# The gate products of a token mixer taken out of the mixer and run between the steps of gated linear attention

## Chip, cores, metric

One core of one Trainium2 chip. The metric is the device time of one execution in microseconds, the median of several executions.

## What is computed

One layer of a bidirectional encoder on 512 prompt tokens and 2048 sample tokens (2560 together, width 1024, all in f32). The part that matters here:

```python
(aq, ak, av, gq, gk, gv, gr, glf, glb, ga, gg) = split_cols(h @ p['w_in'][l])
attn = windowed_gqa(...)
la_f = jax.nn.log_sigmoid((glf @ p['gla_wa2_fwd'][l] + p['gla_ba_fwd'][l])) / GLA_GATE_NORMALIZER
la_b = ...                                    # the same for the other direction
o_f = gla_chunked(gq, gk, gv, la_f, False)
o_b = gla_chunked(gq[:, ::-1], gk[:, ::-1], gv[:, ::-1], la_b[:, ::-1], True)[:, ::-1]
o_g = rms_norm(o_f + o_b, p['gla_norm'][l]).reshape(B, S, GLA_VAL_WIDTH) * jax.nn.silu(gr)
merged = (jax.nn.sigmoid(ga) * (attn @ p['w_branch_attn'][l])
          + jax.nn.sigmoid(gg) * (o_g @ p['w_branch_gla'][l]))
return merged @ p['w_out'][l]
```

`ga` and `gg` are 1024 wide each: two products of `h` with 1024 columns of `w_in`. They need `h` alone, neither the attention nor its result. After this come a norm, the residual sum, a router and 16 experts.

## The kernel before

The kernel is written engine by engine: each phase is a block in which every engine (PE the matrix engine, ACT, DVE, POOL, and SP, which issues most loads) has its own list of instructions, run strictly in the order of the code; semaphores are the only ties between engines. Phases: the front (norm and modulation, `hT` stored), projections and windowed attention (`pa_`), gated linear attention (`gla_`), the mixer (`mix_`), routing, experts (`moe_`), the final norm.

An f32 product of full precision is written as three products of `fp32r` parts (`product3`, lines 103 to 105): high by high, high by low, low by high. So each weight and each input gets a high part (`w_hi`, `a_hi`: a cast on ACT) and a low part (`w_lo`, `a_lo`: raw minus high, on DVE).

`phase_gla` runs first backward over the tiles of 128 tokens (18 steps: a scan on DVE, exponentials on ACT, a turn of the keys and a product on PE, the state on DVE, kept in `Sb`), then forward over 20 tiles (slots). A slot of the forward pass on DVE: the scan of the next tile's decays (L1170), 24 small subtractions that make the arguments of the exponentials (`args`, L1139 to L1143), the state's arguments (L1179, L1180), the norm of the last output (L1201), five predicated copies that pick the levels out of PSUM (`level`, L1195), the product with q (`times_q`, L1186), the state (L1240) and the final product (L1208). ACT makes the exponentials (`exps`, L1257 to L1260), POOL the product with k (`times_k`, L1301), the mean squares' power (`rms`) and the store of `og`. PE makes the levels (L1362, L1371), the turn of the keys (L1379), the state's product (L1389) and the output (L1396 to L1402). Two PSUM tiles `p_g` take the levels in turn.

`phase_mix` runs over five blocks of 512 tokens in 20 chunks of weights each. Even chunks below 16 hold two pieces of 128 columns of `w_in` (for `ga` and `gg`, 48 products 512 wide), odd ones the two branch matrices (24 products 512 wide); chunks 16 to 19 hold 256 columns of `w_out` each (96 products 256 wide). ACT takes the sigmoid of the gates out of PSUM (L1610), DVE multiplies by the branches (L1695), sums (L1697), and the merged tile is split into `m_hi` (ACT, L1617) and `m_lo` (DVE, L1699). The norm, residual sum, squares, turn and router product of block b-1 (`post_a`, `post_b`, `post_c`) are spread over the chunks of block b. Weights have two buffers, `w_raw[m % 2]`: chunk m+1 is split while chunk m runs.

Of the kernel before, what the change touches and what calls it, by code (L numbers as in the profile page):

```python
# [14 lines left out]
P = 128  # L15
# [868 lines left out]
def phase_gla(nc, K, I, S):  # L884

# [4 lines left out]
    NG = NLEV - DIRECT  # L897
    with Mem(nc, "gla") as M:
# [6 lines left out]


# [14 lines left out]


        p_g = [M.ps(f"p_g{i}", [P, 2, 2, 2, P]) for i in range(2)]
# [3 lines left out]
        p_k, p_s = p_ks[:, 0:2], p_ks[:, 2:4]  # L927
        PAIRS = (NG + 1) // 2
        DVE_LEVELS = 6
        s_c, s_m, s_z = M.sem("consts_loaded"), M.sem("mask_step"), M.sem("zeroed")  # L930

# [13 lines left out]
        f_st = [M.sem(f"f_stored{i}") for i in range(2)]  # L945

        def toks(t):
            return bass.ds(t * P, P)
# [9 lines left out]

        with nc.Block() as block:
            @block.sync  # L960
            def _(sp):
                with nc.allow_non_contiguous_dma(reason="a small vector onto partitions"):
                    sp.dma_start(gnorm[:], I["gla_norm"].rearrange("b p -> p b")).then_inc(s_c, 16)
                sp.wait_ge(s_c, 16)

            @block.gpsimd
            def _(pool):
                pool.iota(ip[:], pattern=[[0, P]], base=0, channel_multiplier=1)
                pool.iota(it[:], pattern=[[1, P]], base=0, channel_multiplier=0).then_inc(s_m, 1)
                pool.memset(L[:], 0.0)  # L970

# [16 lines left out]
        with nc.Block() as block:  # L988
            def tiles(eng, tile):

                tile(0, 19, 0)
                tile(1, 18, 1)
                with eng.Fori(1, 7) as i:
                    tile(i * 2, 19 - i * 2, 0)
                    tile(i * 2 + 1, 18 - i * 2, 1)
                for n, t in ((14, 5), (15, 3), (16, 2), (17, 1)):
                    tile(n, t, n % 2)

            p_u = (p_o[:, 0], p_o[:, 1])

            @block.gpsimd
            def _(pool):
                pool.memset(Sf[:], 0.0)

            def is_left(n):

                return not isinstance(n, int) or n < 18

            @block.sync
            def _(sp):  # L1010
                def load_lk(n, t, u):
                    wait(sp, b_B, n - 1)
                    held(sp, K)
                    sp.dma_start(L[:, u, 2:4, 1:P + 1], S["la"][2:4, :, toks(t)].rearrange("c p n -> p c n")).then_inc(b_in[u], 16)
                    wait(sp, b_k, n - 1)
                    held(sp, K)
                    sp.dma_start(k[:, u], S["gk"][:, :, toks(t)].rearrange("c p n -> p c n")).then_inc(b_kin[u], 16)

                def tile(n, t, u):
                    if isinstance(n, int) and n == 0:  # L1020
                        load_lk(0, t, 0)
                    if is_left(n + 1):
                        load_lk(n + 1, 3 if isinstance(n, int) and n == 14 else t - 1, 1 - u)
                    wait(sp, b_p, n - 1)
                    held(sp, K)
                    sp.dma_start(v[:, u], S["gv"][toks(t), :]).then_inc(b_v[u], 16)
                tiles(sp, tile)

            @block.vector
            def _(dve):  # L1030
                def sums(n, u):
                    dve.wait_ge(b_in[u], (n - u) * 8 + 16)
                    wait(dve, b_e, n - 1)
                    dve.tensor_tensor_scan(B[:, u, 2:4].rearrange("p c n -> p (c n)"),
                                           keep[:, 2:4].rearrange("p c n -> p (c n)"),
                                           L[:, u, 2:4].rearrange("p c n -> p (c n)"), 0.0, ALU.mult, ALU.add).then_inc(b_B, 1)
# [76 lines left out]
        with nc.Block() as block:  # L1113
            def slots(eng, slot, last=None):
# [3 lines left out]
                if last:  # L1118
                    last()
# [1314 lines left out]
```

## Time and profile before

| | |
|---|---|
| median of 3 executions | 4129.35 us (4125.22 to 4130.35) |
| the profiled execution: time, span | 4131.49 us, 4129.9 us |
| PE busy | 3618.6 us (88%) |
| DVE busy | 2144.4 us (52%) |
| ACT busy | 1551.2 us (38%) |
| POOL busy | 478.6 us (12%) |
| mean granted clock of PE | 0.918 |
| bytes by DMA | 592.61 MB, mean 143 GB/s |

Busy times are sums over the whole span, and the stages differ: which engine a stage waits for has to be read stage by stage. The granted clock is a share of 2.4 GHz; 0.50 is the lower of its two levels, 1.2 GHz, and values between are means of both. Lengths of matmuls overlap; the pace of a run of them is read from start to start.

### The profile page before, as it was taken

The numbers are of one execution on the slowest core, as the hardware profiler recorded it, in microseconds if no ns is written. First come the engines' busy times: TensorE is split into PE (matmuls) and PEld (weight loads), VectorE is DVE, ScalarE is ACT, GpSimd is POOL, SyncE is SP. The second block draws the span as 40 slices with busy tenths as digits, with TensorE's granted clock in tenths as the row PEclk, the third lists the DMA queues.
The fourth block names the chain that finished last, engine by engine and source line by source line (L and its number), as shares of the span: only waits on it lengthen the run. The fifth ranks groups of instructions, "written<-read, shape, count | busy, mean of one in ns | idle before, by whom it ended". The sixth has DMA issues, their size and how long they took to land. (4 is left out here: it accounts for less than half of the span.)

```text
span 4129.9 us, 60082 instructions
## 1 busy us (share of the span) xinstructions
PE 3618.6 (88%) x22692; PEld 3049.2 (74%) x22692; DVE 2144.4 (52%) x3948; ACT 1551.2 (38%) x2274; POOL 478.6 (12%) x571
## 2 busy tenths in 40 slices
PE   7699999996566589999999963999999999999990
PEld 3377776764345478888888852999999999999990
DVE  1334444554899733444344425555555656555544
ACT  2334544553333233343334220444433443444442
POOL 0000100000344300000000010001000111010003
PEclk9799999997676789999999965999999999999995
DMA  8633343323222244454454432555555555555548
GB/s 286 226 118 104 104 130 97 104 88 97 80 78 65 79 114 143 130 156 138 133 153 143 148 130 72 164 167 171 168 161 164 157 173 169 164 180 160 165 135 328
DMA packets 537807, 592.61 MB, mean 143 GB/s; under 512 B 75640, under 2 KB 450456, under 8 KB 536736
## 3 DMA queue, kind: packets, MB, share of 16 engines
q1 hardware_dynamic: 506896, 474.84, 36.9%
q0 software_dynamic: 30016, 104.88, 8.3%
q10 hardware_dynamic: 720, 10.49, 0.6%
q8 instruction: 119, 1.95, 0.2%
q14 instruction: 56, 0.46, 0.0%
HBM read 484.23 MB, written 105.91 MB: 143 GB/s over the span
## 5 line engine op out<-in xcount | busy, mean ns | idle before, releaser
L103 PE MATMUL moe_pg<-moe_x_hi,moe_w_hi 128*128 128x320 f32 x2048 | 635.1, 310 | 1.4 <-DVE moe_x_lo L2195 1.4
L105 PE MATMUL moe_pg<-moe_x_hi,moe_w_lo 128*128 128x320 f32 x2048 | 633.4, 309 | 0.0
L104 PE MATMUL moe_pg<-moe_x_lo,moe_w_hi 128*128 128x320 f32 x2048 | 633.4, 309 | 0.0
L2157 DVE TENSOR_TENSOR moe_w_lo<-moe_w_raw,moe_w_hi 128x2048 fp32r<-128x2048 f32 x192 | 439.9, 2291 | 370.8 <-ACT moe_w_hi L2105 314.2
L1635 DVE TENSOR_TENSOR mix_w_lo<-mix_w_raw,mix_w_hi 128x2048 fp32r<-128x2048 f32 x100 | 186.4, 1864 | 493.4 <-ACT mix_w_hi L1560 493.4
L2105 ACT CAST moe_w_hi<-moe_w_raw 128x2048 fp32r<-128x2048 f32 x192 | 364.6, 1899 | 172.6 <-DMA moe_w_raw<-in_w_gate_e_dram 95.7
L103 PE MATMUL mix_pu<-mix_a_hi,mix_w_hi 128*128 128x512 f32 x960 | 380.4, 396 | 21.3 <-DVE mix_w_lo L1635 9.3
L103 PEld LDWEIGHTS moe_pg<-moe_x_hi,moe_w_hi 128*128 128x128 f32 x2048 | 385.1, 188 | 2.4 <-issue 1.5
L104 PEld LDWEIGHTS moe_pg<-moe_x_lo,moe_w_hi 128*128 128x128 f32 x2048 | 385.1, 188 | 0.6
L105 PEld LDWEIGHTS moe_pg<-moe_x_hi,moe_w_lo 128*128 128x128 f32 x2048 | 385.0, 188 | 0.0
L105 PE MATMUL mix_pu<-mix_a_hi,mix_w_lo 128*128 128x512 f32 x960 | 376.3, 392 | 0.0
L104 PE MATMUL mix_pu<-mix_a_lo,mix_w_hi 128*128 128x512 f32 x960 | 376.2, 392 | 0.0
L103 PE MATMUL pa_pu<-pa_h_hi,pa_w_hi 128*128 128x512 f32 (+1 forms) x560 | 227.9, 407 | 37.7 <-DVE pa_h_lo L644 37.7
L103 PEld LDWEIGHTS mix_pu<-mix_a_hi,mix_w_hi 128*128 128x128 f32 x960 | 182.0, 190 | 62.0 <-DVE mix_w_lo L1635 11.4
L104 PE MATMUL pa_pu<-pa_h_lo,pa_w_hi 128*128 128x512 f32 (+1 forms) x560 | 220.7, 394 | 0.0
L105 PE MATMUL pa_pu<-pa_h_hi,pa_w_lo 128*128 128x512 f32 (+1 forms) x560 | 220.6, 394 | 0.0
L105 PEld LDWEIGHTS mix_pu<-mix_a_hi,mix_w_lo 128*128 128x128 f32 x960 | 181.8, 189 | 38.6
L104 PEld LDWEIGHTS mix_pu<-mix_a_lo,mix_w_hi 128*128 128x128 f32 x960 | 182.1, 190 | 37.1
L103 PE MATMUL moe_pd<-moe_w_hi,moe_h_hi 128*128 128x512 f32 x512 | 203.2, 397 | 0.0
L105 PE MATMUL moe_pd<-moe_w_hi,moe_h_lo 128*128 128x512 f32 x512 | 199.7, 390 | 0.0
L104 PE MATMUL moe_pd<-moe_w_lo,moe_h_hi 128*128 128x512 f32 x512 | 199.5, 390 | 0.0
L103 PE MATMUL mix_pu<-mix_w_hi,mix_m_hi 128*128 128x256 f32 x640 | 182.2, 285 | 2.1 <-DVE mix_m_lo L1699 2.1
(309 smaller groups left out, 7104.1 us busy)
## 6 DMA issues: line engine op xcount, KB each, us to landing
moe_w_raw<-in_w_gate_e_dram SPq DMA_DIRECT2D x64, 1024.0 KB
moe_w_raw<-in_w_up_e_dram SPq DMA_DIRECT2D x64, 1024.0 KB
moe_w_raw<-in_w_down_e_dram SPq DMA_DIRECT2D x64, 1024.0 KB
mix_w_raw<-in_w_in_dram SPq DMA_DIRECT2D x80, 512.0 KB
pa_w_raw<-in_w_in_dram SPq DMA_DIRECT2D x35, 1024.0 KB
front_w<-in_w_ada_dram SPq DMA_DIRECT2D x24, 1024.0 KB, 11.8
mix_w_raw<-in_w_out_dram SPq DMA_DIRECT2D x20, 1024.0 KB
scratch_hT<-front_hT ACTq DMA_DIRECT2D x5, 2048.0 KB, 10.4
```

The costliest lines, as they stand in the source:

```text
L103: pe.matmul(out, w_hi, x_hi, start=start, stop=False)
L104: pe.matmul(out, w_hi, x_lo, start=False, stop=False)
L105: return pe.matmul(out, w_lo, x_hi, start=False, stop=stop)
L1635: dve.tensor_tensor(w_lo[:, m % 2, 0:n], w_raw[:, m % 2, 0:n], w_hi[:, m % 2, 0:n].bitcast(F32), ALU.subtract).then_inc(s_wlo, 1)
L2105: act.copy(w_hi[:, m % 2], w_raw[:, m % 2]).then_inc(s_whi, 1)
L2157: dve.tensor_tensor(w_lo[:, m % 2], w_raw[:, m % 2], w_hi[:, m % 2].bitcast(F32), ALU.subtract).then_inc(s_wlo, 1)
```

## The change

The 80 gate products (5 blocks, 8 column pieces, `ga` and `gg`) are taken out of the mixer. In `phase_gla` each is a `unit(n)` of 24 products, 512 wide, with `h` split once for a block and its 128 columns of weights split by ACT and DVE. Units 0 to 18 stand in the backward pass, one a step; unit 19 between the passes; three in each slot of the forward pass. ACT copies each unit out of PSUM (`read_unit`), POOL stores it to a scratch tensor `gate`. PSUM for this comes from the levels: `p_g` is now one tile. The subtractions, levels and norms of a slot on DVE are in another order, with the low parts of the weights between them, and the output of tile t-1 is made in slot t. The passes and the blocks of the mixer are written out, without register loops.

The mixer has 12 chunks a block: 8 with both branch matrices (24 products 512 wide) and 4 that hold half of the rows for 512 columns of `w_out` (48 products 512 wide). The gates are read back by SP into `sg`, 128x1024 at a time in two slots, and ACT takes the sigmoid in SBUF. `post_a` is at even branch chunks, `post_b` at odd ones.

```diff
+        def load_w(sp, n):
...
+            wait(sp, d_wlo, n - 1)
+            c0 = (C_GA, C_GG)[n % 2] + n % 16 // 2 * P
+            sp.dma_start(w_raw[:, n % 2], win[:, :, c0:c0 + P]).then_inc(d_w[n % 2], 16)
+        def load_h(sp, i):
+            wait(sp, d_hlo, 2 * i - 4)
...
+                def after_unit(n):
+                    if ends_block(n):
+                        split_h_lo(dve, (n + 1) // 16)
+                    split_w_lo(dve, n + 3)
...
+                for t in range(NT):
+                    n, w = FIRST_U + PER * t, 1 - t % 2
+                    more = t + 1 < NT
+                    if more:
+                        sums(t + 1)
+                        args(dve, w, 0)
+                        args(dve, w, 1)
+                    after_unit(n)
+                    level(t, 0)
+                    if more:
+                        args(dve, w, 2)
+                        args(dve, w, 3)
+                    if t:
+                        norm(t - 1)
+                    after_unit(n + 1)
+                    level(t, 1)
+                    level(t, 2)
+                    if more:
+                        args(dve, w, 4)
+                        args(dve, w, 5)
+                        state_args(t + 1)
+                    state(t)
+                    after_unit(n + 2)
+                    level(t, 3)
+                    level(t, 4)
+                    if t:
+                        final(t - 1)
+                    if more:
+                        times_q(t + 1)
...
+                def read_unit(n):
+                    act.wait_ge(d_u, n + 1)
+                    wait(act, d_st[n % SG], 16 * (n // SG))
+                    act.copy(sg[:, n % SG], pd[n % 2][:]).then_inc(d_ev, 1)
+                    if ends_block(n):
+                        split_h_hi(act, (n + 1) // 16)
+                    split_w_hi(act, n + 3)
...
+                    read_unit(n + 1)
+                    if t + 1 < NT:
+                        exps(t + 1)
+                    read_unit(n + 2)
...
+                for t in range(NT):
+                    n = FIRST_U + PER * t
+                    unit(n)
+                    if t:
+                        out(t - 1)
+                    pe.wait_ge(f_x, t + 1)
+                    pe.wait_ge(f_xq, t + 1)
+                    levels(t, 0)
+                    turn_keys(t)
+                    unit(n + 1)
+                    levels(t, 1)
+                    state_product(t)
+                    unit(n + 2)
+                    levels(t, 2)
+                    if t:
+                        turn_out(t - 1)
...
-    NM, NUB = 20, 40
+    NM, NUB = 12, 24
...
+                def load_gate(b, c):
+                    g = b * KD + c
...
+                    wait(sp, s_mlo, g - 1)
+                    sp.dma_start(sg[:, g % 2], S["gate"][2 * c:2 * c + 2, :, b * BLK:(b + 1) * BLK].rearrange("c p n -> p c n"))\
+                        .then_inc(s_g[g % 2], 16)
...
+                        load_w(b * NM + m + 2)
+                        if b and m in (1, 3):
+                            load_x(b - 1, (m + 3) // 2)
+                        if m < 6:
+                            load_gate(b, m + 2)
...
+                        split(b * NM + m + 1)
+                        if m < 8:
+                            g = b * KD + m
+                            if m < 7:
+                                gate(b, m + 1)
+                            if m == 0 and b:
+                                squares(b - 1)
+                            if b and m in (3, 5, 7):
+                                post_b(b - 1, (m - 3) // 2)
+                            act.wait_ge(s_mg, g + 1)
...
+                            act.copy(m_hi[:, m], sg[:, g % 2, 0]).then_inc(s_mhi, 1)
+                            if b and m % 2 == 0:
+                                post_a(b - 1, m // 2)
```

How this stands in the engines' queues at two places. ACT in a slot of the forward pass, before (one slot and the start of the next; `gla_A` is the copy of level 0, `gla_X` the exponentials):

```order
L1266 ACTIVATE gla_junk,gla_ss<-gla_p_o 128x128 x4
L1278 COPY gla_A<-gla_p_g 128x512
L1281 COPY gla_kdT<-gla_p_ks 128x256
L1257 ACTIVATE gla_X<-gla_X 128x2048
L1258 ACTIVATE gla_dec<-gla_B 128x4
L1259 ACTIVATE gla_X<-gla_B 128x256
L1260 ACTIVATE gla_X<-gla_X 128x2048
```

The same slot of the change (`gla_sg` is the copy of a gate unit out of PSUM, `gla_w_hi` the high part of the weights three units on):

```order
L1357 ACTIVATE gla_junk,gla_ss<-gla_p_o 128x128 x4
L1370 COPY gla_A<-gla_p_g 128x512
L1375 COPY gla_kdT<-gla_p_ks 128x256
L1307 COPY gla_sg<-gla_pd 128x512
L992 CAST gla_w_hi<-gla_w_raw 128x1024
L1347 ACTIVATE gla_X<-gla_X 128x2048
L1348 ACTIVATE gla_dec<-gla_B 128x4
L1349 ACTIVATE gla_X<-gla_B 128x256
L1350 ACTIVATE gla_X<-gla_X 128x2048
L1307 COPY gla_sg<-gla_pd 128x512
L992 CAST gla_w_hi<-gla_w_raw 128x1024
```

The copy and the high part of the second unit stand ahead of the exponentials, those of the third behind them.

DVE at the end of a slot, before (from the state's arguments to the next scan):

```order
L1179 TENSOR_TENSOR gla_X<-gla_B 128x256
L1180 TENSOR_TENSOR gla_X<-gla_B 128x256
L1201 TENSOR_TENSOR gla_on<-gla_p_o,gla_rstd 128x2x2x128
L1195 COPY_PREDICATED gla_A<-gla_mask,gla_p_g 128x512 x5
L1186 TENSOR_TENSOR gla_X<-gla_X,gla_q 128x2304
L1240 SCALAR_TENSOR_TENSOR gla_Sf<-gla_Sf,gla_dec,gla_p_ks 128x128 x2
L1208 SCALAR_TENSOR_TENSOR gla_og<-gla_p_f,gla_gnorm,gla_gr 128x512
L1170 SCALAR_TENSOR_TENSOR gla_B<-gla_keep,gla_L 128x516
```

And of the change (first slot, which has no final product yet):

```order
L1217 TENSOR_TENSOR gla_X<-gla_B 128x256
L1218 TENSOR_TENSOR gla_X<-gla_B 128x256
L1260 SCALAR_TENSOR_TENSOR gla_Sf<-gla_Sf,gla_dec,gla_p_ks 128x128 x2
L998 TENSOR_TENSOR gla_w_lo<-gla_w_raw,gla_w_hi 128x1024
L1232 COPY_PREDICATED gla_A<-gla_mask,gla_p_g 128x512 x2
L1224 TENSOR_TENSOR gla_X<-gla_X,gla_q 128x2304
L1207 SCALAR_TENSOR_TENSOR gla_B<-gla_keep,gla_L 128x516
```

The low part of the third unit's weights now stands between the state and the last two levels. In the mixer, SP over three branch chunks of the second block, before:

```order
L1499 DMA mix_w_raw<-in_w_branch_gla_dram 128x4x128
L1499 DMA mix_w_raw<-in_w_in_dram 128x8x128 x2
L1535 DMA mix_x<-in_x_prompt_dram 128x1024
L1499 DMA mix_w_raw<-in_w_branch_attn_dram 64x4x128 x2
L1499 DMA mix_w_raw<-in_w_branch_gla_dram 128x4x128
```

And of the change (`mix_sg` is the gate that is read back):

```order
L1670 DMA mix_sg<-scratch_gate 128x2x512
L1654 DMA mix_w_raw<-in_w_branch_attn_dram 64x4x128
L1655 DMA mix_w_raw<-in_w_branch_attn_dram 64x4x128
L1656 DMA mix_w_raw<-in_w_branch_gla_dram 128x4x128
L1681 DMA mix_x<-in_x_prompt_dram 128x1024
L1670 DMA mix_sg<-scratch_gate 128x2x512
```

The load of a gate, which waits for the merge two chunks before, stands ahead of the next weights.

## Rows read from the trace of the kernel before

**Rows 1.** Windows: stretch, length, engines busy (instructions), granted clock share, DMA share, GB/s.

```profile
700.00:970.00 270.00, 266.56 (x1467) 190.85 (x1466) 141.32 (x360) 143.98 (x270) 25.06 (x40) 1.00 0.30 94
996.00:1050.00 54.00, 32.26 (x180) 18.41 (x180) 28.61 (x72) 14.79 (x54) 0.00 (x0) 0.50 0.59 171
1053.00:1399.00 346.00, 209.24 (x2472) 167.18 (x2472) 315.44 (x692) 114.48 (x256) 153.47 (x148) 0.72 0.23 69
1453.00:2411.00 958.00, 938.17 (x5184) 817.63 (x5184) 384.78 (x362) 328.32 (x394) 35.32 (x72) 0.99 0.45 135
2025.00:2030.00 5.00, 0.72 (x3) 0.51 (x3) 0.00 (x0) 4.62 (x8) 0.00 (x0) 0.73 0.04 7
2030.00:2035.00 5.00, 5.00 (x15) 3.86 (x14) 3.33 (x3) 1.49 (x3) 1.22 (x2) 0.58 0.10 28
```

**Rows 2.** PE timeline, 512-wide products; the second row is 32 starts later.

```profile
1654.89 0.39 PE L103 MATMUL mix_pu<-mix_a_hi,mix_w_hi 128*128 128x512 f32 x1
...
1662.14 0.39 PE L105 MATMUL mix_pu<-mix_a_hi,mix_w_lo 128*128 128x512 f32 x1
```

**Rows 3.** PE timeline, 256-wide products; the second row is 56 starts later.

```profile
1799.72 0.28 PE L103 MATMUL mix_pu<-mix_w_hi,mix_m_hi 128*128 128x256 f32 x1
...
1806.44 0.28 PE L105 MATMUL mix_pu<-mix_w_hi,mix_m_lo 128*128 128x256 f32 x1
```

**Rows 4.** PE timeline, one tile of the forward pass.

```profile
1208.72 0.71 PE L1396 MATMUL gla_p_o<-gla_v,gla_A 128*128 128x128 f32 x4 [0.80 <-DVE gla_A L1195]
...
1210.97 0.39 PE L1402 MATMUL gla_p_o<-gla_Sb,gla_X 64*128 64x128 f32 x4
1212.23 0.71 PE L1362 MATMUL gla_p_g<-gla_X 64*128 64x128 f32 x8 [0.87 <-issue]
...
1214.58 1.16 PE L1362 MATMUL gla_p_g<-gla_X 64*128 64x128 f32 x16
```

**Rows 5.** DVE timeline, the same stretch.

```profile
1203.62 2.47 DVE L1195 COPY_PREDICATED gla_A<-gla_mask,gla_p_g 128x512 f32<-128x512 int32 x3
...
1208.56 3.58 DVE L1186 TENSOR_TENSOR gla_X<-gla_X,gla_q 128x2304 f32<-128x2304 f32 x1
...
1212.57 0.74 DVE L1208 SCALAR_TENSOR_TENSOR gla_og<-gla_p_f,gla_gnorm,gla_gr 128x512 f32<-128x512 f32 x1
1213.23 1.22 DVE L1170 TENSOR_TENSOR_SCAN gla_B<-gla_keep,gla_L 128x516 f32<-128x516 f32 x1
...
1215.01 0.48 DVE L1140 TENSOR_TENSOR gla_X<-gla_B 128x128 f32<-128x128 f32 x1
...
1220.27 0.28 DVE L1143 TENSOR_TENSOR gla_X<-gla_B 128x128 f32<-128x128 f32 x1
```

**Rows 6.** ACT timeline, the same stretch.

```profile
1203.13 1.91 ACT L1257 ACTIVATE gla_X<-gla_X 128x2048 f32<-128x2048 f32 x1 [4.45 <-DVE gla_X L1180]
...
1205.35 1.89 ACT L1260 ACTIVATE gla_X<-gla_X 128x2048 f32<-128x2048 f32 x1
```

**Rows 7.** DVE timeline, a later block of the mixer.

```profile
1841.47 1.22 DVE L1635 TENSOR_TENSOR mix_w_lo<-mix_w_raw,mix_w_hi 128x1024 fp32r<-128x1024 f32 x1 [10.73 <-ACT mix_w_hi L1560]
1842.61 1.28 DVE L1647 SCALAR_TENSOR_TENSOR mix_mix<-mix_mix,mix_r,c_gate 128x1024 f32<-128x1024 f32 x1
...
1852.88 1.28 DVE L1695 TENSOR_TENSOR mix_sg<-mix_sg,mix_pu 128x512 f32<-128x512 f32 x2
1854.19 0.69 DVE L1697 TENSOR_TENSOR mix_sg<-mix_sg 128x512 f32<-128x512 f32 x1
```

**Rows 8.** ACT timeline, the same block.

```profile
1840.40 1.03 ACT L1560 CAST mix_w_hi<-mix_w_raw 128x1024 fp32r<-128x1024 f32 x1
1841.86 0.60 ACT L1610 ACTIVATE mix_sg<-mix_pu 128x512 f32<-128x512 f32 x1 [0.42 <-PE mix_pu L105]
```

**Rows 9.** DMA issues: count, KB each, median us to landing.

```profile
mix_a_raw<-scratch_oa SPq DMA_DIRECT2D x10, 512.0 KB, 3.9
mix_a_raw<-scratch_og SPq DMA_DIRECT2D x10, 512.0 KB, 4.8
```

More of the change, by code:

```diff
@@ L1113, in phase_gla @@
-        with nc.Block() as block:
-            def slots(eng, slot, last=None):
-                for t in range(NT):
-                    slot(t, t % 2)
-                if last:
-                    last()
-            def is_tile(t, n):
-                return isinstance(t, int) and t == n
-            def lv(t, u, per):
-                return (t - u) * (per // 2) + per
             def args(eng, u, j):
@@ L1331, in last @@
-                def last():
-                    rms(NT - 1, 1)
-                    store(NT - 2, 0)
-                    store(NT - 1, 1)
-                    for u in range(2):
-                        pool.wait_ge(f_st[u], 8 * NT)
-                slots(pool, slot, last)
+                    pool.dma_start(S["og"][:, :, toks(t)].rearrange("c p n -> p c n"), og[:, t % 2]).then_inc(f_st[t % 2], 16)
+                for n in range(FIRST_U - 1):
+                    store_gate(n)
+                pool_args(0)
@@ new lines, in _ @@
+                split(0)
+                for i in range(4):
+                    split_a(0, i)
+                for b in range(NB):
+                    for m in range(NM):
+                        split(b * NM + m + 1)
+                        if m < 8:
+                            merge(b, m)
+                        if b and m % 2 == 0 and m < 8:
+                            post_a(b - 1, m // 2)
+                        if b and m % 2 == 1 and m < 8:
+                            post_b(b - 1, m // 2)
+                        if b and m in (5, 7, 9, 11):
+                            post_c(b - 1, (m - 5) // 2)
+                        if m >= 8 and b < NB - 1:
@@ new lines, in out @@
+                def out(b, n, kh):
+                    s = (b * NM + 8 + 2 * n + kh) % 2
+                    for t in range(TPB):
+                        u = b * NUB + 16 + 4 * n + t
+                        if kh == 0:
+                            read(pe, u)
+                        ts = slice(t * P, (t + 1) * P)
+                        for k in range(4 * kh, 4 * kh + 4):
+                            if n == 0 and t == 0:
+                                pe.wait_ge(s_mlo, b * KD + k + 1)
+                            ws = slice(k % 4 * 512, k % 4 * 512 + 512)
+                            mm = product3(pe, bank(u)[:], m_hi[:, k, ts], m_lo[:, k, ts], w_hi[:, s, ws], w_lo[:, s, ws],
+                                          k == 0, k == KD - 1)
+                        if kh == 1:
+                            mm.then_inc(s_u, 1)
+                    if kh == 0:
+                        mm.then_inc(s_half, 1)
```

933 lines of the change are left out of this document (495 added, 438 removed).

## The prediction

> **What bounds the kernel now.** I read the busy time by stretches first [rows 1]. The mixer (1453 to 2411 us) is five blocks of 191.6 us, and there PE is busy 938 of 958 us at a granted clock of 0.99: it is bound by PE. Before it the gated linear attention takes the backward pass (996 to 1050) and the forward pass (its scans 1052 to 1398, so 18.2 us a tile). In the forward pass DVE is busy 315 of 346 us and PE 209, at clock 0.72; in the backward pass PE runs at 0.50. So the change moves work from a stretch that PE bounds into one where PE has room and DVE has nearly none. The gain is not the moved work but what the attention doesn't give back.
>
> **The work that moves.** A product 512 wide starts every 7.25/32 = 0.2266 us [rows 2], one 256 wide every 6.72/56 = 0.120 us [rows 3]. A gate unit is 24 products of 512: 5.44 us. There are 80 of them, 435 us of PE at 2.4 GHz. The output product goes from 1920 products of 256 to 960 of 512: 230.4 - 217.5 = 13 us saved, no more.
>
> **The backward pass.** A step of its own is 32.3/18 = 1.8 us of PE at half clock [rows 1], so 0.9 to 1.0 beside a unit that brings the full clock: 6.4 us a step. ACT then has per unit a copy out of PSUM (0.5) and a high part (1.03) [rows 8], DVE a low part (1.14, from start to start) [rows 7]; both fit under 6.4. The first unit waits for the parts of h, of which the fourth is only loaded when a slot is free, and runs partly at half clock: 17 us until it and its turn are done. 17 further steps make 109, the split of h for unit 16 about 4, the last step and hand-overs 8. Sum 138 against 54: **+84**.
>
> **The forward pass** is a chain around a slot (one tile, three units). PE in a slot: 16.3 for units, 2.6 for the output (1208.72 to the end of the run at 1210.97) [rows 4], 3.5 for the levels and keys that start at 1212.23 and end at 1215.7, and 2.8 for the last level, state product and turn, which stand at half clock before: 25.2 us. DVE is 16.6 (315 of 346, by 18.2) plus three low parts, 20.0. Neither is the sum, because the engines are in order. DVE now has, before levels 3 and 4, the low part of the third weight, and ACT makes its high part only after the exponentials of the next tile and after the third unit's copy. I follow the loop from DVE's product with q:
>  - product with q 3.5 [rows 5]; PE level 0 and keys 2.5 with hand-over; the second unit 5.6 with its drain; ACT copy and high part 1.6; DVE low part 1.2: 14.4;
>  - levels 1 and 2 1.5, arguments 1.6 (eight at 0.20), state arguments 0.75 [rows 5]; exponentials 4.1 (1203.13 to 1207.2) [rows 6]; copy and high part 1.6; low part 1.2: 10.75;
>  - levels 3 and 4 1.5, the final product 0.66 [rows 5]: 2.2.
> Sum 27.35, and 0.35 for POOL's product with k running beside the low part (arguments take 0.48 beside POOL and 0.28 alone [rows 5]): **27.7 us a slot**, with PE idle 0.6 us before the output and some 1.7 before level 0. 19 of them are 526. The first tile needs its sums, arguments, exponentials and product with q before level 0: 19. The last from its level 0 to the last store: 30.5. Three of the four later block boundaries fall here (units 31, 47, 63): high and low parts of h queue ahead of the weights, and the fourth piece is loaded only after the first two low parts, with a landing like 3.9 to 4.8 us [rows 9]: 1.8 + 4.5 + 1.1 = 7.4 each, 22. Clock after the longer gaps: 5. Sum 602.5 against 1050 to 1437, 387: **+215.5**.
>
> **The mixer** keeps 24 products for each of eight branch chunks (5.44 us), but now a second loop stands beside PE. The gate of chunk m+1 may be loaded only when chunk m-1 is merged (two slots of sg), and ACT takes its sigmoid before it makes m_hi of chunk m. Merge to merge: SP and landing 4.5 (512 KB in rows of 2 KB, 3.9 and 4.8 [rows 9]), sigmoid of 1024 columns 1.07 (a cast of 1024 columns 1.03 [rows 8]), m_hi 0.65, m_lo 0.75: **7.0**, over PE's 5.44. In blocks 1 to 4 after an even chunk, DVE has the two operations of the norm (2.45) and ACT the squares (1.1) ahead of the next high part (1.05); then low part 1.15, two products 1.3, sum 0.7 [rows 7], m_hi and m_lo 1.45: 9.2. PE then idles over 4 us, and a gap like that was followed by 0.58 of the clock for 5 us (2025 to 2035 us) [rows 1], about 2.3 us lost, so after an odd chunk I take 7.4 instead of 7.0. Block: first merge 8.8 (the unit, then squares of the last block), 3 x 9.2 + 3 x 7.4 = 49.8, the wait for the first 2048-column weight of the output 7.8, its 192 products 43.5, transposes and router products that fall there 4.3, half clock 1.5: 115.7. First block, with a shorter start: 14 + 6 x 7.0 + 3.4 + 43.5 = 103. Sum 103 + 4 x 115.7 = 566 against 958: **-392**. The five blocks at PE's own pace would be some 490, so I expect 75 of the gain to be lost to this loop. The router constants ahead and the post of the last block behind stay.
>
> **Sum.** 84 + 215.5 - 392 = -92.5. The profiled execution took 4131.5, so 4039; it stands 2.1 above the median of the three, so **4037 us**. The added loads and stores of the gates (21 MB each way) lie under it: in the forward pass DMA is at 0.23 now, in the mixer at 0.45 [rows 1]. Were they not hidden, 42 MB at the 300 GB/s that 135 at a share of 0.45 means would be 140 us.
>
> **The clock, the rule that speaks against.** From 700 to 970 PE is busy with pauses and small products between wide ones, and the clock is 1.00; in the forward pass with 0.60 busy it is 0.72 [rows 1]. 25.2 of 27.7 is nearer the first, so I take the full clock. The Trainium skill (TensorE: Matmul & The Clock Gate, "A second HAM failure mode: psum-queue depth-cycling") tells of a kernel whose short pauses between groups kept the clock going to and fro. By that rule the third rival would be the forecast, and the sum positive.
>
> **The rivals.**
>  - *The loops are looser than I drew them.* Slots at PE's 25.2 give -48; the mixer at 490 gives -76. Together 3913. For it: landings of 3.9 are the lower of the two, and PE is the classic bound. Against: the order in each queue is fixed in the program. 10%.
>  - *The loops are tighter.* Slots of 31 us (arguments at 0.48 rather than 0.28 would add 4.8 with POOL's three more stores per tile) give +63, and landings of 5.5 in the mixer with traffic of x1, xn and weights beside them +1 on each of 39 merges, +39. That takes 102 away: 4139, no gain. Half of this way is likelier than all of it. 16% for a clear part of it, of which 4 within 0.2%, 3 beyond.
>  - *Slower: PE at half clock in the forward pass.* A slot costs PE 25.2 (1 + f) us if a share f of its work runs at 1.2 GHz. At f = 0.5 it is 37.8, +10.1 over 27.7, times 19 = +192: 4229. It decides from 32.6 us a slot, f = 0.29. For it: 0.72 now, and the waits that each slot keeps. Against: the stretch from 700 on. 11%.
>  - *The change doesn't do what it says* is no case here: the products are the same in number and the order shows them moved.
>
> **How the numbers follow.** The forecast has 63%, with 3990 to 4085 as its own range (slots of 26.5 to 29.5, merges 0.8 us either way). With the rivals, 3965 to 4125 leaves out the full half-clock case, most of the looser one and the end of the tighter one, 2 in 10. Faster by over 0.2% (8 us, about what a measurement of this kernel can tell): 0.63 + 0.10 + 0.09 and a little of the clock case = 0.83. Within: 0.04. Slower: 0.13.
>
> **What would show it.** The forward scans 27 to 28 us apart, with DVE waiting once per tile for w_hi behind the exponentials; PE's clock near 1.0 from the second unit on; ACT waiting for the gate's load in most branch chunks, and merges 7 and 9 us apart in turn; out products starting 0.227 apart; the mixer near 566 + 15 + 42. Wrong it would be if scans stood 32 us apart, if PEclk there were under 0.8, or if branch chunks ran at 5.5 us.

## The result, and the profile after

The changed kernel takes 4135.58 us (median, 4127.37 the fastest) against 4124.07 us for the kernel before in the same session: ratio 1.0031, 95% interval 1.0021 to 1.0041. It is slower by 0.3%, where 4037 us had been forecast, and it lies above both stated ranges (3990 to 4085, and 3965 to 4125). One of the twenty executions of the changed kernel took 4359.68 us at a granted clock of 0.81 and is left out of the ratio.

Windows of the changed kernel: backward pass with its start, forward pass, mixer, everything behind; columns as in [rows 1]. They run from POOL's first instruction of the gated linear attention (973.4) over the first scan of the forward pass (1167.7) and the first load of the mixer (1757.8) to ACT's squares behind the last output product (2409.8).

```profile
973.40:1167.70 194.30, 143.29 (x668) 109.94 (x669) 70.27 (x124) 56.89 (x112) 12.09 (x23) 0.87 0.55 164
1167.70:1757.80 590.10, 510.96 (x4114) 406.29 (x4112) 406.81 (x821) 223.04 (x423) 215.07 (x221) 0.96 0.45 132
1757.80:2409.80 652.00, 547.57 (x2336) 452.41 (x2336) 276.31 (x310) 235.23 (x298) 35.30 (x72) 0.88 0.49 153
2409.80:4133.00 1723.20, 1512.44 (x9872) 1389.25 (x9872) 968.15 (x1810) 640.41 (x787) 203.05 (x218) 0.92 0.53 169
```

The same events in the kernel before (985.5, 1052.1, 1437.5, 2411.5, and the end at 4129.9) give these windows:

```profile
985.50:1052.10 66.60, 32.26 (x180) 18.41 (x180) 35.29 (x87) 16.07 (x55) 1.86 (x4) 0.50 0.52 150
1052.10:1437.50 385.40, 229.10 (x2680) 182.79 (x2680) 338.91 (x739) 122.61 (x280) 165.11 (x160) 0.72 0.23 68
1437.50:2411.50 974.00, 945.56 (x5216) 824.84 (x5216) 390.60 (x370) 332.59 (x397) 35.32 (x72) 0.98 0.46 135
2411.50:4129.90 1718.40, 1511.24 (x9872) 1387.76 (x9872) 968.35 (x1810) 640.48 (x787) 201.56 (x218) 0.92 0.53 170
```

| stretch | before | after | change | forecast | off by |
|---|---|---|---|---|---|
| ahead of the attention's passes | 985.5 | 973.4 | -12 | 0 | -12 |
| backward pass | 66.6 | 194.3 | +128 | +84 | +44 |
| forward pass | 385.4 | 590.1 | +205 | +215.5 | -11 |
| mixer | 974.0 | 652.0 | -322 | -392 | +70 |
| behind it | 1718.4 | 1723.2 | +5 | 0 | +5 |

The first row is no gain of the change. The code ahead of `phase_gla` is the same in both kernels, and in the thirteen profiled executions of this case the phase starts either at 972 to 975 us (five of them) or at 982 to 986 (eight), with no edit ahead of it: the kernel before was profiled in the second group, the changed kernel in the first. So stretches are compared here by their lengths, and single times between two traces can be off by some 10 us. The stages that the change touches, with the one behind them, are 15 us longer in the traces, where the ratio says 13. Against the -92.5 of the forecast they miss by 108 us.

Two thirds of that is the mixer, where PE is busy 548 of 652 us at a clock of 0.88, after 946 of 974 at 0.98. Where its idle time lies is read from PE's groups in blocks 1 to 4 of the mixer (lines view; the last part is the idle time ahead of a group and what ended it):

```profile
L103 PE MATMUL mix_pu<-mix_a_hi,mix_w_hi 128*128 128x512 f32 x240 | 106.4, 443 | 14.6 <-DVE mix_w_lo L1802 14.6
L103 PE MATMUL mix_pu<-mix_w_hi,mix_m_hi 128*128 128x512 f32 x256 | 105.7, 413 | 0.0
...
L1917 PE MATMUL mix_p_l<-mix_wra,mix_xT 128*128 128x16 f32 x256 | 48.0, 335 | 72.3 <-DVE c_logit L1842 59.9 <-DVE mix_w_lo L1802 9.3 <-ACT mix_xT L1748 3.1
```

The branch products, which the loop of the forecast was to hold up, hardly wait: 14.6 us. The router product, 16 columns wide, carries 72.3 us of the idle time, 59.9 of it (eight waits, two a block) for c_logit, which is DVE's read of the logits of the tile before. One such place on PE's timeline, and DVE beside it:

```profile
2057.38 0.39 PE L105 MATMUL mix_pu<-mix_a_hi,mix_w_lo 128*128 128x512 f32 x1
2064.29 3.57 PE L1917 MATMUL mix_p_l<-mix_wra,mix_xT 128*128 128x16 f32 x16 [6.52 <-DVE c_logit L1842]
2067.70 0.77 PE L103 MATMUL mix_pu<-mix_a_hi,mix_w_hi 128*128 128x512 f32 x1
...
2075.28 1.03 PE L1909 MATMUL mix_p_x<-c_ident,mix_xn 128*128 128x128 f32 x8
```

```profile
2060.02 1.28 DVE L1816 TENSOR_TENSOR mix_sg<-mix_sg,mix_pu 128x512 f32<-128x512 f32 x2
2061.33 0.69 DVE L1818 TENSOR_TENSOR mix_sg<-mix_sg 128x512 f32<-128x512 f32 x1
2062.71 0.69 DVE L1820 TENSOR_TENSOR mix_m_lo<-mix_sg,mix_m_hi 128x512 fp32r<-128x512 f32 x1 [0.68 <-ACT mix_m_hi L1768]
2063.32 0.75 DVE L1837 TENSOR_SCALAR mix_xn<-mix_mix,mix_r 128x1024 f32<-128x1024 f32 x1
2063.98 0.17 DVE L1842 TENSOR_TENSOR c_logit<-mix_p_l,mix_rb 128x16 f32<-128x16 f32 x1
```

DVE reads the logits (0.17 us of work) only behind the merge of the chunk before, since they stand there in its list. PE may not write the next logits into the one PSUM tile `p_l` until then, and the chunk behind it stands behind that router product. So chunks 6 and 8 of each of these blocks start one whole merge late (ahead of chunk 4 the router product waits 3.1 us, for the weights' low part or its own input, ahead of chunk 10 not at all). The router product then takes 3.41 us (2064.29 to 2067.70) and the chunk 7.58 (2067.70 to 2075.28). With the router product moved, in the first experiment below, it takes 1.7 us, and a chunk in which the clock did not fall 5.62.

PE's windows over this place (columns as above, the granted clock third from the end) show why: the clock was 0.50 over the router product and the start of the chunk, and full again in the next chunk.

```profile
2064.30:2067.70 3.40, 3.40 (x17) 3.40 (x17) 0.98 (x1) 0.63 (x1) 0.60 (x1) 0.50 0.89 265
2067.70:2071.00 3.30, 3.30 (x9) 2.63 (x10) 0.00 (x0) 0.43 (x1) 0.00 (x0) 0.50 0.94 301
...
2076.00:2081.00 5.00, 5.00 (x25) 4.17 (x24) 3.97 (x5) 0.86 (x2) 0.00 (x0) 1.00 0.00 0
```

### The profile page after: what moved, and what is told of

Read it like the earlier page. It is cut to its first block and busy times, and to the rows that moved or that the text cites. A ratio compares the mean times of both kernels' runs of the same rounds, so it can differ in the third digit from the quotient of the medians.

```text
span 4133.0 us, 57570 instructions
## 1 busy us (share of the span) xinstructions
PE 3602.4 (87%) x21732; PEld 2983.3 (72%) x21732; DVE 2132.7 (52%) x4008; ACT 1594.8 (39%) x2374; POOL 540.3 (13%) x651
## 5 line engine op out<-in xcount | busy, mean ns | idle before, releaser
L103 PE MATMUL gla_pd<-gla_h_hi,gla_w_hi 128*128 128x512 f32 x640 | 265.4, 415 | 41.2 <-DVE gla_h_lo L1011 39.5
L105 PE MATMUL gla_pd<-gla_h_hi,gla_w_lo 128*128 128x512 f32 x640 | 256.3, 400 | 0.0
L104 PE MATMUL gla_pd<-gla_h_lo,gla_w_hi 128*128 128x512 f32 x640 | 256.1, 400 | 0.0
L1802 DVE TENSOR_TENSOR mix_w_lo<-mix_w_raw,mix_w_hi 128x1024 fp32r<-128x1024 f32 (+1 forms) x60 | 94.8, 1580 | 224.3 <-ACT mix_w_hi L1717 224.3
L998 DVE TENSOR_TENSOR gla_w_lo<-gla_w_raw,gla_w_hi 128x1024 fp32r<-128x1024 f32 x80 | 116.2, 1454 | 162.4 <-ACT gla_w_hi L992 162.3
L2249 POOL DMA_INDIRECT scratch_y<-moe_ys,moe_isc x48 | 78.1, 1628 | 853.3 <-ACT moe_ys L2311 731.4
L2300 ACT CAST moe_h_hi<-moe_hd 128x320 fp32r<-128x320 f32 x128 | 58.9, 460 | 312.6 <-DVE moe_hd L2388 312.6
L103 PEld LDWEIGHTS gla_pd<-gla_h_hi,gla_w_hi 128*128 128x128 f32 x640 | 124.5, 194 | 72.3 <-DVE gla_w_lo L998 30.0
```

Of the source, the lines that this page charges most:

```text
L103: pe.matmul(out, w_hi, x_hi, start=start, stop=False)
L104: pe.matmul(out, w_hi, x_lo, start=False, stop=False)
L105: return pe.matmul(out, w_lo, x_hi, start=False, stop=stop)
L998: dve.tensor_tensor(w_lo[:, n % WB], w_raw[:, n % 2], w_hi[:, n % WB].bitcast(F32), ALU.subtract).then_inc(d_wlo, 1)
L1802: dve.tensor_tensor(w_lo[:, g % 2, 0:n], w_raw[:, g % 2, 0:n], w_hi[:, g % 2, 0:n].bitcast(F32), ALU.subtract).then_inc(s_wlo, 1)
L2249: pool.indirect_dma_start(out=S["y"], out_offset=bass.IndirectOffsetOnAxis(ap=isc[0:ROWS[r], r:r + 1], axis=0), in_=ys[0:ROWS[r], r], in_o ...
```

## The experiments

Two theories on the mixer: **T1**, the router product's place in PE's list, with the read it waits for; **T2**, the forecast's own loop of the gates read back (two slots, each load behind a merge). **T3** is on the backward pass (the order of SP's loads), **T4** on the forward pass (the order of ACT's work), **T5** on DVE's work beside POOL's. Gains in us below are differences of ratios times 4124; every kernel was compared with the kernel before on its own chip.

**Router product behind the chunk.**

```diff
-                        if b and m in (4, 6, 8, 10):
-                            post_b(b - 1, (m - 4) // 2)
                         if m < 8:
                             branches(b, m)
                         else:
                             out(b, (m - 8) // 2, m % 2)
+                        if b and m in (4, 6, 8, 10):
+                            post_b(b - 1, (m - 4) // 2)
```

> One edit in the mixer on TensorE: the router product of the block before (post_b) is issued behind the branch chunk m = 4, 6, 8, 10 instead of ahead of it. Theory T1 (router product): in the changed kernel TensorE stood 6.52 and 8.44 us ahead of router products, waiting for VectorE's read of the logits, which comes only behind the merge of the chunk before, and the chunk behind the router product then ran at 7.7 us instead of 5.44. If that is the loss of blocks 1 to 4, their spacing falls from about 131 us to 112 to 118, the waits of the router product lie under a chunk, and the time falls by 50 to 75 us, to a ratio to before of 0.985 to 0.991. Theory T2 (the loop of the gate read-back, two slots of which each is loaded only behind a merge): the chain merge, load, sigmoid, high part stays as it is, and the time moves by less than 10 us. Both: the GLA stage is not touched and takes what it took, 985 to 1752.

Ratio 0.9865 (0.9848 to 0.9882): 68 us under the changed kernel. The mixer in its trace takes 576 us (1765.3 to 2341.4, by the same events) instead of 652, at a clock of 0.95. From block to block it takes 113 to 117 us instead of 133 to 135. PE's groups of blocks 1 to 4:

```profile
L103 PE MATMUL mix_pu<-mix_a_hi,mix_w_hi 128*128 128x512 f32 x253 | 105.7, 418 | 30.8 <-DVE mix_w_lo L1802 30.8
L103 PE MATMUL mix_pu<-mix_w_hi,mix_m_hi 128*128 128x512 f32 x256 | 104.0, 406 | 12.8 <-DVE mix_w_lo L1802 12.8
...
L1917 PE MATMUL mix_p_l<-mix_wra,mix_xT 128*128 128x16 f32 x256 | 29.6, 257 | 0.0
```

The wait for the logits is gone, and the router products themselves fall from 48.0 to 29.6 us, because they no longer follow a gap with the clock at 0.50. Of the 72.3 us 29 come back as a wait for the weights' low part (43.6 instead of 14.6, and none ahead of router products). T1 holds; ACT's wait for the gate loads stayed (65.5 us against 64.5). A second PSUM tile for the logits should lift the same wait without the move; no run tried it.

**Three gate slots.** The edit's core; `sg`, its semaphores and the slot numbers go from two to three with it.

```diff
...
-                    wait(sp, s_mlo, g - 1)
+                    wait(sp, s_mlo, g - 2)
...
-                        if m < 6:
-                            load_gate(b, m + 2)
+                        if m < 5:
+                            load_gate(b, m + 3)
...
```

> One edit in the mixer: three slots for the gates read back instead of two, so that each load is issued one chunk earlier (SyncE waits for the merge before the last one). Theory T2 (gate loop): a load lands 4.1 us after its issue and ScalarE waited 64.5 us in 20 waits for it; with a slot more the loads are there, and the time falls by 40 to 75 us. Theory T1 (router product in TensorE's order): ScalarE's waits for the gate load vanish, but the even chunks are still held behind the router product, whose logit read comes behind a merge; the merges come perhaps 1 to 3 us earlier in a few chunks, so that the time falls by 0 to 20 us, and the waits of 6 to 8 us for the logit read stay in TensorE's rows.

Ratio 1.0026 (1.0012 to 1.0039), the changed kernel's own. Alone, the third slot is worth nothing. ACT's waits show where the time went, first in the changed kernel, then here (us in total, times, longest):

```profile
ACT mix_m_hi L1768 <- DVE mix_sg L1818: 95.1, 31, 8.9
...
ACT mix_sg L1728 <- DMA mix_sg<-scratch_gate: 64.5, 20, 4.0
```

```profile
ACT mix_m_hi L1769 <- DVE mix_sg L1819: 154.9, 36, 12.7
```

The wait for the load falls from 64.5 us to 0.8, and the next wait of the same engine grows by 59.8. Merges (DVE's L1818, from one to the next) tell the same: in the third block they stand 9.5, 6.9, 9.1, 11.0, 9.1, 14.9 and 11.0 us apart in the changed kernel, and with three slots the third block has the same seven within 0.1 us. The two that hold the router products, 11.0 (into chunk 4) and 14.9 (into chunk 6), are the ones that shrank when these moved, to 5.5 and 5.3. T2 falls as the cause of the miss.

**Both edits.** Router product behind the chunk and three slots.

> Router product behind the chunk and three gate slots, the backward pass as in the changed kernel. It tells what the third slot is worth once the router product no longer holds the chunks: if the gate loop (T2) is the next limit, 15 to 30 us under the kernel with the router product's move alone; if all three edits simply add, the third slot gives what it gave alone, nothing, and the gain of the three edits came from elsewhere.

Ratio 0.9824 (0.9805 to 0.9843): 17 us under the router edit alone. The mixer takes 560 us (1762.2 to 2322.1), 16 less. So the landing of the gates is a limit behind the router product, and taking it out is worth 17 us. What a third slot cannot take out stays: PE still waits 36.9 us for the weights' low part, whose high part ACT makes only behind the merge.

**Weight loads of the backward pass one step later.**

```diff
-                load_w(sp, 5)
                 for n in range(NBW):
...
-                    load_w(sp, n + 6)
+                    load_w(sp, n + 5)
...
+                load_w(sp, NBW + 5)
                 load_L(0)
```

> One edit in the backward pass of the gated linear attention, on SyncE: the weight loads of the gate product run one step later (unit n + 5 behind step n instead of n + 6, and the load of unit 23 ahead of the forward pass's first). Theory T3 (order of SyncE): in the changed kernel the loads of the decay matrix, the keys and the values stood behind a weight load that waited for the low part of unit n + 4, so that the scan waited 4.7 us for the decay matrix in every other step and steps went 6.4 and 8.5 us in turn; now the weight load's slot is free when SyncE reaches it, all steps take 6.4 to 6.8 us, the stretch from the second block to the first forward scan falls from 183 us to 145 to 155, and the time by 25 to 35 us. Rival: the weights now come late, TensorE waits for the split of the weights in each step instead, and the stretch gains under 10 us or loses. The mixer is not touched.

Ratio 0.9956 (0.9941 to 0.9971): 31 us under the changed kernel. DVE's scans (L1158) in the changed kernel, over four steps, then here, over five:

```profile
1021.72 0.70 DVE L1158 TENSOR_TENSOR_SCAN gla_B<-gla_keep,gla_L 128x258 f32<-128x258 f32 x1 [4.74 <-DMA gla_L<-scratch_la]
...
1048.30 0.70 DVE L1158 TENSOR_TENSOR_SCAN gla_B<-gla_keep,gla_L 128x258 f32<-128x258 f32 x1 [4.57 <-DMA gla_L<-scratch_la]
1055.58 0.70 DVE L1158 TENSOR_TENSOR_SCAN gla_B<-gla_keep,gla_L 128x258 f32<-128x258 f32 x1 [4.62 <-DMA gla_L<-scratch_la]
```

```profile
1023.34 0.70 DVE L1158 TENSOR_TENSOR_SCAN gla_B<-gla_keep,gla_L 128x258 f32<-128x258 f32 x1 [2.27 <-DMA gla_L<-scratch_la]
...
1049.18 0.69 DVE L1158 TENSOR_TENSOR_SCAN gla_B<-gla_keep,gla_L 128x258 f32<-128x258 f32 x1 [1.42 <-DMA gla_L<-scratch_la]
1055.65 0.70 DVE L1158 TENSOR_TENSOR_SCAN gla_B<-gla_keep,gla_L 128x258 f32<-128x258 f32 x1 [1.45 <-DMA gla_L<-scratch_la]
```

In the changed kernel four steps take 33.9 us, 8.5 each; here five steps take 32.3, 6.46 each, which is the forecast's 6.4. Over thirteen steps, with a block boundary among them, it is 8.2 against 6.9. The cause stands in SP's list: the load of the weights waits for a slot, and the decay matrix L is issued only behind it (start, us, what):

```profile
1001.51 7.05 SPq L979 DMA_DIRECT2D gla_w_raw<-in_w_in_dram  x3
1008.61 0.58 SPq L1080 DMA_DIRECT2D gla_v<-scratch_gv  x1
1009.23 0.48 SPq L1074 DMA_DIRECT2D gla_L<-scratch_la  x1
...
1026.61 0.37 SPq L979 DMA_DIRECT2D gla_w_raw<-in_w_in_dram  x1
1027.03 0.58 SPq L1080 DMA_DIRECT2D gla_v<-scratch_gv  x1
1027.65 0.43 SPq L1074 DMA_DIRECT2D gla_L<-scratch_la  x1
```

From the first backward scan to the first forward scan it takes 150.9 us here (995.1 to 1146.0) and 181.3 in the changed kernel (986.5 to 1167.7), 30 more, as the times say. T3 holds.

**The three edits together.**

> The three edits together: router product behind the chunk, three gate slots, weight loads of the backward pass one step later. By T1 with T3 the time falls by 50 to 75 us from the first, 25 to 35 from the third and 0 to 10 from the second, in all 80 to 115 us under the changed kernel, a ratio to before of 0.975 to 0.983. If T2 is right and T1 not, the sum of the three edits is that of the second and the third. If the gate loop is what stands behind the router product as the next limit, the sum is more than the single edits give.

Ratio 0.9738 (0.9719 to 0.9757): 121 us under the changed kernel, a little over the upper end, since the third slot is worth 17 behind the router edit and none alone. Against both mixer edits the backward edit gives 35, as alone (31).

**The width of the output product**, two products of 256 for each of 512:

```diff
-                            mm = product3(pe, bank(u)[:], m_hi[:, k, ts], m_lo[:, k, ts], w_hi[:, s, ws], w_lo[:, s, ws],
-                                          k == 0, k == KD - 1)
+                            for q0 in (0, 256):
+                                wq = slice(k % 4 * 512 + q0, k % 4 * 512 + q0 + 256)
+                                mm = product3(pe, bank(u)[:, q0:q0 + 256], m_hi[:, k, ts], m_lo[:, k, ts],
+                                              w_hi[:, s, wq], w_lo[:, s, wq], k == 0 and q0 == 0, k == KD - 1 and q0 == 256)
```

> The changed kernel with its output product 256 columns wide again: each of the 960 matmuls of 512 columns is issued as two of 256. The forecast's term: two at 0.120 us against one at 0.2266, so 0.0134 us each, 960 of them: the time rises by 13 us over the changed kernel if TensorE sets the pace of the output phase. Rival: the output phase waits for the weights' low part anyway, and the width moves the time by less than 4 us.

Ratio 1.0064 (1.0046 to 1.0083): 13.6 us over the changed kernel, by the difference of the middles (the intervals, 1.0021 to 1.0041 and 1.0046 to 1.0083, leave 2 to 26). In its trace the mixer takes 661 us instead of 652, with the same waits of PE. The forecast's term of 13 agrees with the middle; its rival, under 4 us, is unlikely but not shut out.

**Third unit read ahead of the exponentials** (forward pass, ACT):

```diff
+                    read_unit(n + 2)
                     if t + 1 < NT:
                         exps(t + 1)
-                    read_unit(n + 2)
```

> One edit in the forward pass of the changed kernel, on ScalarE: the read of the slot's third gate unit and the high part that follows it stand ahead of the four exponentials of the next step instead of behind them. In the changed kernel VectorE waits 5.09 us in every ordinary slot for that high part, and a slot takes 26.92 us. Theory T4 (this order bounds the slot): the high part is there 2.1 us earlier at least, its subtraction no longer lies beside GpSimd's key product (1.21 us instead of 2.19), the exponentials end 1.5 to 2.5 us later and the query product with them; the slot falls to 24 to 26 us and the 20 slots by 20 to 50 us. Rival: the slot is bound by exponentials, key product and query product in a row, which now start later, and the time rises by 10 to 30 us. The mixer is not touched.

Ratio 0.9988 (0.9975 to 1.0002): 18 us under the changed kernel, and one slot 25.89 us instead of 26.92: a little under the 20 to 50 that T4 gave, so T4 holds in kind and not in size. What took the rest back is on DVE: the product with q, 2.55 us in the changed kernel, now lies beside POOL's product with k. Its row and POOL's:

```profile
1386.33 4.85 DVE L1224 TENSOR_TENSOR gla_X<-gla_X,gla_q 128x2304 f32<-128x2304 f32 x1 [0.74 <-ACT gla_X L1350]
```

```profile
1384.17 4.59 POOL L1400 TENSOR_TENSOR gla_X<-gla_X,gla_k 128x2048 f32<-128x2048 f32 x1 [9.37 <-ACT gla_X L1347]
```

They overlap for 2.43 us (1386.33 to 1388.76), and DVE's product is 2.30 longer. The changed kernel shows the same (DVE's rows first, then POOL's); there the low part is the operation that grows:

```profile
1377.38 2.19 DVE L998 TENSOR_TENSOR gla_w_lo<-gla_w_raw,gla_w_hi 128x1024 fp32r<-128x1024 f32 x1 [5.09 <-ACT gla_w_hi L992]
...
1381.59 2.55 DVE L1224 TENSOR_TENSOR gla_X<-gla_X,gla_q 128x2304 f32<-128x2304 f32 x1
...
1387.76 1.21 DVE L998 TENSOR_TENSOR gla_w_lo<-gla_w_raw,gla_w_hi 128x1024 fp32r<-128x1024 f32 x1
```

```profile
1373.87 4.61 POOL L1400 TENSOR_TENSOR gla_X<-gla_X,gla_k 128x2048 f32<-128x2048 f32 x1 [7.13 <-ACT gla_X L1347]
```

1.10 us of overlap (1377.38 to 1378.48), and the low part is 2.19 instead of 1.21. Both times DVE gained next to nothing while POOL's product ran. That is T5: DVE's operations with two inputs stand still beside it.

**The product with k on DVE**, in the place where DVE waited 5.09 us. `times_k` has the same body, with `dve` for `pool`; POOL's calls are taken out, and DVE makes the first tile's product ahead of the loop.

```diff
...
                     state(t)
+                    if more:
+                        times_k(t + 1)
                     after_unit(n + 2)
...
```

> The changed kernel with the forward pass's key product on VectorE instead of GpSimd, in the place where VectorE stands idle 5.09 us in every ordinary slot (between the state update and the low part of the third unit). Theory T5 (VectorE's two-input operations stand still while GpSimd's key product runs): the low part, which took 2.19 us where 1.12 us of it lay beside the key product, takes 1.21; the key product takes 2.3 us on VectorE (2048 elements at the 2.55 us that the query product has for 2304) and lies in the idle time; the slot falls from 26.92 us to 25.9 and the 20 slots by 15 to 22 us. Rival T6: the longer low part is the weights' own (a fresh landing, another reader), and VectorE only gets 2.3 us more: the low part stays at 2.19 and the time within 5 us.

Ratio 0.9983 (0.9969 to 0.9998): 20 us under the changed kernel. DVE in one slot:

```profile
1374.14 2.29 DVE L1225 TENSOR_TENSOR gla_X<-gla_X,gla_k 128x2048 f32<-128x2048 f32 x1 [1.53 <-ACT gla_X L1358]
1377.70 1.23 DVE L998 TENSOR_TENSOR gla_w_lo<-gla_w_raw,gla_w_hi 128x1024 fp32r<-128x1024 f32 x1 [1.26 <-ACT gla_w_hi L992]
...
1380.95 2.55 DVE L1232 TENSOR_TENSOR gla_X<-gla_X,gla_q 128x2304 f32<-128x2304 f32 x1
1383.42 1.23 DVE L1207 TENSOR_TENSOR_SCAN gla_B<-gla_keep,gla_L 128x516 f32<-128x516 f32 x1
```

The product takes 2.29 us instead of POOL's 4.61, the low part 1.23 instead of 2.19, and the scans stand 25.95 us apart instead of 26.92. T5 holds, T6 (a low part that is slow by itself) falls: of the 80 low parts none is over 1.228 us here, where 19 were over 1.3 and the longest was 2.492.

**And the third unit read between the first exponential and the second:**

```diff
...
+                    if between is not None:
+                        read_unit(between)
                     act.activation(dec[:, u], B[:, u, :, P], ACT.Exp, scale=1.0 / 16)
...
```

> As the kernel with the key product on VectorE, and on ScalarE the read of the third unit with its high part stands between the first exponential and the second instead of behind all four. If the chain exponentials, high part, low part, levels, query product bounds the slot, the low part starts 1.3 us earlier and the slot falls to between 24.8 and 25.9 us; TensorE's own work in a slot is 25.0 us (26.92 less its idle 1.41 and 0.48), so that it can't go far below: 20 to 40 us under the changed kernel in all. Rival: the second exponential, 1.5 us later, is waited for by the query product, and the slot stays at that of the kernel without the split.

Ratio 0.9915 (0.9891 to 0.9940): 48 us under the changed kernel, more than the 20 to 40 expected. The slot is 24.6 us (scans at 1353.73 and 1378.36). PE is busy through the whole of that slot (24.63 of 24.63 us, at a clock of 1.00), so here the slot is PE's, and the expected floor of 25.0 was 0.4 too high.

**The three edits with an edit of the forward pass.** First with the third unit read ahead of all exponentials:

> All four edits together: router product behind the chunk, three gate slots, weight loads of the backward pass one step later, third unit read ahead of the exponentials in the forward pass. If the fourth gives 20 to 50 us alone, the time is that much under the kernel with the three, a ratio to before of 0.961 to 0.970; if it loses alone, it loses here too.

Ratio 0.9694 (0.9676 to 0.9713), 18 us under the three edits, as alone. Then with the key product on DVE and the third unit read between the exponentials:

> Router product behind the chunk, three gate slots, weight loads of the backward pass one step later, and the key product on VectorE with the third unit read between the exponentials. The parts add: the kernel with the first three stood at 0.9738 of before; less 20 to 40 us this gives 0.964 to 0.969, which is under the 0.9694 of the kernel with the read ahead of all exponentials if T5 holds.

Ratio 0.9634 (0.9610 to 0.9658), 3975 us: 151 us under the kernel before, and just under the expected 0.964 to 0.969. Under the three edits it is 43 us, where the same edit gave 48 alone. It beats both kernels; the order of four lists and one moved product stand between it and the changed kernel, and no product of the gates was moved back.

## Why the prediction was wrong

**The frame was right.** PE's room in the attention takes the gate products at the price that their pace sets (25.0 us busy in an ordinary slot, at a clock of 1.00, where 25.2 had been drawn), and the width of the output product agrees with its 13 us.

**The mixer, -392 (measured -322), is the step that failed.** The prediction counted "transposes and router products that fall there 4.3" as work of the output phase, and drew the branch phase as one loop between merge, gate load and sigmoid. It left out that PE's list has a router product ahead of chunks 4, 6, 8 and 10, and that ahead of 6 and 8 its wait is for a read which DVE makes behind a merge. That is a second loop through PE, one merge long, and its wait is the one that ends last. Its price: 72.3 us of idle time ahead of router products, 18.4 for router products after a gap (48.0 against 29.6), and chunks behind it at 7.58 instead of 5.62. Putting it behind the chunk shortened the mixer by 76 us in the trace and the time by 68. (The whole trace is 70 us shorter, as the two lie in different groups by the first row of the table.)

With this loop gone the mixer takes 576 us, where the forecast had 974 - 392 = 582, and a block 113 to 117 us, where it had 115.7. The merges, which the forecast wanted 9.2 and 7.4 us apart in turn, stand 9.5, 7.0, 9.1, 5.5, 9.8, 5.3 and 11.9 apart (third block), 58.1 together where the forecast has 59.0. So the loop that had been drawn is there, and nearly of its size, once the other is gone. The landing of the gates is the small part of it: of the 75 us of gain that the loop was to cost, a third slot gives 17 back. With it PE is busy 508 us of 560 and still waits 36.9 for the weights' low part, behind work of ACT and DVE between two merges; no run took that apart.

**The backward pass, +84 (measured +128).** The step of 6.4 us was right for the engines and wrong for SP: many steps took 7.3 and 9.1 us in turn (scans at 1039.18, 1048.30, 1055.58 us), and the mean of thirteen was 8.2. The prediction listed PE, ACT and DVE for each step and never followed SP's list, in which the loads of L, v and k stand behind a weight load that waits for a slot. With that load one step later the stretch from scan to scan is 151 us, 30 shorter, where the forecast had 138. The other 13 us lie in uneven steps (8 to 10 us at the start and beside the new parts of h) and in the count of units. Twenty lie in this stretch, and the sum has a first one and 17 steps: units 18 and 19 run from 1132 to 1144 us and the first forward scan starts at 1146, where 8 us stood for the last step and hand-overs.

**The forward pass, +215.5 (measured +205).** The chain was right (DVE waits twice a slot for the high part, 1.93 and 5.09 us) and its length nearly: 26.92 against 27.7. Two of its terms missed in opposite directions. The product with q took 2.55 us, not 3.5: the 3.58 of [rows 5] had POOL's product beside it for 1.15 us (from 1205.18 to 1209.71 in that trace). The low part took 2.19 and not 1.2 plus 0.35, for the same reason. So the near hit on the slot is in part luck. The three block boundaries cost 7.4, 5.7 and 6.7 us more than a slot, where 7.4 each had been taken.

**The rule on the clock that spoke against the change** did not show itself in the forward pass: its granted clock is 0.96, and 1.00 in an ordinary slot, so the rival of a half clock there is out. The half clock came in the mixer instead, with the gaps of 6.5 and 8.4 us (0.50 from 2064.3 to 2071.0, by the windows of the section on the result).

**The rivals.** "The loops are tighter" gave 4139 us, close to the measured time, and would have been right for the wrong reasons: it wanted slots of 31 us and landings of 5.5, and these were 26.92 and 4.1. No rival named an order within a queue that puts a small product ahead of the wide ones, nor SP. Of the signs that the prediction named, the scans came nearly as said and ACT waited for 20 of the 40 gate loads, but the merges stood up to 14.9 us apart. None of its signs of being wrong came (scans 32 us apart, a clock under 0.8, branch chunks at 5.5 us), though the forecast was wrong: they watched only the chains that had been drawn.

## What to carry to other kernels

When work leaves a loop, what is left is held by the small items that the big one used to cover: list every instruction on each in-order queue, SP's too, with what it waits for, and ask of each whether a wide one stands behind it. The place of a 0.17 us read and of a 16-column product cost 68 us here, the gate loads 17. And test a suspected loop by relaxing it alone and together with the other: the third slot gave nothing alone and 17 us once the router product was out of the way.

## What the runs showed of the hardware

A two-input operation of DVE on SBUF makes almost no progress while POOL's product runs, and loses nearly the whole overlap: 2.43 us of overlap cost 2.30, and 1.10 cost 0.98 (rows above; POOL's ends are rough). It is so in every such meeting of POOL's product with k and DVE's product with q or low part: over 20 in the kernel before, 19 in the changed kernel and 20 in the one with the third unit read first, DVE lost 0.87 to 0.95 of the overlap. The kernel before already paid 1.03 us a tile for it. The Trainium skill (SBUF — State Buffer, "SBUF: two separate sides") says that DVE and GpSimd share a pair of ports under an exclusive lock and that the later operation blocks until the first one ends; for a DVE operation with two SBUF inputs against a GpSimd one that reads SBUF, this case's trace agrees. The forecast had read the 0.48 against 0.28 of [rows 5] as a mild slowdown. With the product on DVE, 2.29 us of DVE replaced 4.61 us of POOL during which DVE could do little work of this kind.

PE's clock in the mixer, as rows show it: behind a gap of 3.65 us a chunk of 24 products in the kernel with the router product behind took 7.22 us, behind one of 2.39 us it took 5.62. The granted clock was 0.64 from 2014.1 to 2017.0 and 0.84 from there to 2021.3, and 1.00 from 2030.2 to 2035.8.

```profile
2014.08 0.50 PE L103 MATMUL mix_pu<-mix_a_hi,mix_w_hi 128*128 128x512 f32 x1 [3.65 <-DVE mix_w_lo L1802]
...
2021.30 1.03 PE L1909 MATMUL mix_p_x<-c_ident,mix_xn 128*128 128x128 f32 x8
...
2030.17 0.50 PE L103 MATMUL mix_pu<-mix_a_hi,mix_w_hi 128*128 128x512 f32 x1 [2.39 <-DVE mix_w_lo L1802]
2035.79 1.85 PE L1917 MATMUL mix_p_l<-mix_wra,mix_xT 128*128 128x16 f32 x16
```

What stays open: the stretch behind the mixer was 5 us longer in the one profiled execution, with the same work (9872 matmuls) at the same clock; it was not followed further.
